# A weight-streaming kernel of two transformer blocks: low parts of two weight chunks in one VectorE instruction

## What is computed

```python
h = rms_norm(x, g_mix)
proj = h @ w_in
qa, ka, va, qr, kr, vr, gr, gate_a, gate_r = jnp.split(proj, pts, axis=-1)
oa = moba_attention(rms_norm(heads(qa, A_HEADS), q_gain), rms_norm(heads(ka, A_HEADS), k_gain), heads(va, A_HEADS))
orr = retention(heads(qr, R_HEADS), heads(kr, R_HEADS), heads(vr, R_HEADS))
orr = head_group_norm(orr)... * jax.nn.silu(gr)
merged = jax.nn.sigmoid(gate_a) * (oa @ w_o_attn) + jax.nn.sigmoid(gate_r) * (orr @ w_o_ret)
x = x + merged @ w_out
h2 = rms_norm(x, g_ffn)
g, u = jnp.split(h2 @ w_ffn_in, 2, axis=-1)
return x + (jax.nn.silu(g) * u) @ w_ffn_out
```

## Time and profile before

| | |
|---|---|
| median of three runs | 2584.09 us (2583.65 to 2584.09) |
| profiled execution | 2583.7 us, its span 2581.8 us |
| TensorE matmuls | 2568.1 us busy, 99% |
| TensorE weight loads | 2295.8 us, 89% |
| VectorE | 1634.9 us, 63% |
| ScalarE | 1326.9 us, 51% |
| GpSimd | 57.7 us, 2% |
| DMA | 507.39 MB, mean 197 GB/s |
| granted TensorE clock, mean | 0.999 of full speed |

### The profile page before, as it was taken

One profiled execution on the slowest core, in us unless ns is written; L12 is line 12 of the kernel. 1 busy time (PEld: TensorE's weight loads), 2 busy tenths in 40 slices (PEclk: granted clock), 3 DMA queues, 4 the chain that ended last, 5 costly groups with the idle time before them and its releaser, 6 DMA issues.

```text
span 2581.8 us, 38392 instructions
## 1 busy us (share of the span) xinstructions
PE 2568.1 (99%) x13844; PEld 2295.8 (89%) x13844; DVE 1634.9 (63%) x1721; ACT 1326.9 (51%) x1567; POOL 57.7 (2%) x55
## 2 busy tenths in 40 slices
PE   9999999999999999999999999999999999999998
PEld 8998888888889999999888898998889999998887
DVE  7568755556656656566655567667687776766555
ACT  6446665554445444444444466546564444444444
POOL 0000000000000000000000000000000000000000
PEclk9999999999999999999999999999999999999999
DMA  8666666667666666666666655664666666666664
GB/s 262 206 198 190 182 188 176 199 203 225 198 195 193 203 198 202 199 200 202 200 205 201 206 174 168 179 196 155 197 186 200 201 199 204 197 202 202 204 202 165
DMA packets 232229, 507.39 MB, mean 197 GB/s; under 512 B 15856, under 2 KB 16256, under 8 KB 231504
## 3 DMA queue, kind: packets, MB, share of 16 engines
q1 hardware_dynamic: 230272, 498.53, 63.9%
q0 software_dynamic: 1296, 6.88, 0.8%
q10 hardware_dynamic: 576, 0.82, 0.1%
HBM read 504.07 MB, written 2.10 MB: 196 GB/s over the span
## 4 chain that ended last, share of the span: by engine, by line
PE 99%; DVE 1%; DMA 0%; ACT 0%; SPq 0%; issue 0%; DVEq 0%
PE ps L405 31%; PE ps L414 16%; PE ps L416 16%; PE ps L415 16%; PE ps L406 15%; PE ps L478 1%; PE ps L734 0%; PE ps L727 0%; DMA raw<-w_in 0%; PE ps L797 0%; PE ps L550 0%; PE ps L583 0%; DVE wlo L1426 0%; PE ps L383 0%; PE ps L694 0%; PE ps L563 0%
## 5 line engine op out<-in xcount | busy, mean ns | idle before, releaser
L1426 DVE TENSOR_TENSOR wlo<-raw,whi 128x1024 fp32r<-128x1024 f32 x944 | 1169.8, 1243 | 892.4 <-ACT whi L867 883.0
L867 ACT ACTIVATE whi<-raw 128x1024 fp32r<-128x1024 f32 x943 | 996.3, 1058 | 1203.5 <-PE ps L406 597.7
L405 PE MATMUL ps<-hT,whi 128*128 128x512 f32 x3680 | 1208.6, 383 | 1.3 <-DVE hT L1475 0.6
L406 PE MATMUL ps<-hT,wlo 128*128 128x256 f32 x3680 | 1003.1, 273 | 0.0
L405 PEld LDWEIGHTS ps<-hT,whi 128*128 128x128 f32 x3680 | 695.5, 189 | 99.1 <-DVE hT L1475 1.5
L406 PEld LDWEIGHTS ps<-hT,wlo 128*128 128x128 f32 x3680 | 706.5, 192 | 0.2
L414 PE MATMUL ps<-whi,hT 128*128 128x512 f32 x1088 | 420.6, 387 | 0.0
L416 PE MATMUL ps<-whi,hT 128*128 128x512 f32 x1088 | 412.4, 379 | 0.0
L415 PE MATMUL ps<-wlo,hT 128*128 128x512 f32 x1088 | 412.3, 379 | 0.0
L414 PE MATMUL ps<-whi,split_e 128*128 128x512 f32 x832 | 316.2, 380 | 0.0
L415 PE MATMUL ps<-wlo,split_e 128*128 128x512 f32 x832 | 315.3, 379 | 0.0
(11 more groups left out here) (264 smaller groups left out, 1008.0 us busy)
## 6 DMA issues: line engine op xcount, KB each, us to landing
raw<-w_ffn_in SPq DMA_DIRECT2D x352, 512.0 KB, 4.2
raw<-w_in SPq DMA_DIRECT2D x303, 512.0 KB, 4.2
raw<-w_ffn_out SPq DMA_DIRECT2D x176, 512.0 KB, 4.6
raw<-w_o_ret SPq DMA_DIRECT2D x32, 512.0 KB, 4.7
raw<-w_out SPq DMA_DIRECT2D x32, 512.0 KB, 4.6
raw<-w_o SPq DMA_DIRECT2D x32, 512.0 KB, 4.0
raw<-w_o_attn SPq DMA_DIRECT2D x16, 512.0 KB, 4.6
resid<-x POOLq DMA_DIRECT2D x1, 2048.0 KB, 11.9
```

The costliest lines, as they stand in the source:

```text
L405: pe.matmul(acc, whi[:, c % SLOTS, f], in_turn(hT[:, kt, :, :]), start=(kt == 0), stop=False)
L406: mm = pe.matmul(acc[:, 0:SEQ], wlo[:, c % SLOTS, f], in_turn(hT[:, kt, 0, :]), start=False, stop=(kt == KT - 1))
L867: act.activation(whi[:, c % SLOTS, :], raw[:, c % SLOTS, :], ACT.Copy).then_inc(hi_ready, 1)
L1426: dve.tensor_tensor(wlo[:, c % SLOTS, :], raw[:, c % SLOTS, :], whi[:, c % SLOTS, :].bitcast(F32), ALU.subtract).then_inc(lo_ready, 1)
```

## The change

`ahead` on VectorE makes the low parts in twos. `split_two` waits until both high parts are there, makes 2048 columns with one instruction, and adds 2 to `lo_ready` when it ends, so both chunks are signalled to TensorE, and both raw slots to SyncE, at that moment. The pairs are (4, 5) and (6, 7) of this block and (0, 1) and (2, 3) of the next, made at the odd steps. `side` of the even step, which stood between the two splits, now stands ahead of both. With `hold`, step 6 is a single split, and the held one stays where it was. ScalarE, TensorE, GpSimd and SyncE have the same programs as before. In the changed file every line from the new function on stands 8 further down.

```diff
+            def split_two(blk, c):
+                dve.wait_ge(hi_ready, blk * CPB + c + 2)
+                two = slice(c % SLOTS, c % SLOTS + 2)
+                dve.tensor_tensor(wlo[:, two, :], raw[:, two, :], whi[:, two, :].bitcast(F32), ALU.subtract).then_inc(lo_ready, 2)
+
             def ahead(blk, side=nothing, more=True, hold=False):
 
                 side(-1)
                 for k in range(CPB):
                     if k < SLOTS:
-                        split(blk, k + SLOTS)
-                    elif more and not (hold and k == CPB - 1):
+                        if k % 2:
+                            split_two(blk, k - 1 + SLOTS)
+                    elif more and hold and k == CPB - 2:
                         split(blk + 1, k - SLOTS)
+                    elif more and not (hold and k == CPB - 1) and k % 2:
+                        split_two(blk + 1, k - 1 - SLOTS)
                     side(k)
```

## The result

| | before | changed |
|---|---|---|
| median | 2584.05 us (5 runs, 2583.35 to 2584.09) | 2611.7 us (5 runs, 2610.26 to 2612.17) |
| ratio | | 1.0108, 95% interval 1.0097 to 1.0119 |
| profiled execution | 2583.7 us, span 2581.8 | 2610.3 us, span 2608.4 |

The change costs 27.65 us, 1.1%. I had forecast 2601.7 us with a range of 2590 to 2611: the right way, with a loss of 17.6 instead of 27.65, and the measured time lies 0.7 above the range. The profiled execution is the fastest of the five, 26.6 us behind the one of before; it is the one that the traces explain. What makes the other executions up to 1.9 us longer is taken up at run e13, and stays open in part.

The account below looks back on a forecast made before the run. TensorE bounds the kernel, with VectorE's waits as slack. Places of 13.75 us and GpSimd's product of 3.9 add 17.6 to the profiled 2583.7, and the median lies 0.4 above: 2601.7 us, range 2590 to 2611.

Parts of the forecast that it names:

- What bounds the kernel, and the time of the instruction: TensorE bounds, busy 2568.1 of 2581.8 us, VectorE's waits are slack; the instruction of 2048 columns takes 2.29 us.
- The places: Single spots where TensorE misses a low part or a product behind a pair; their losses add to 13.75 us.
- Start: At the kernel's start chunk 4's low part comes with chunk 5's, at 21.6 instead of 19.33: +2.3 us.
- attention's output: Chunks 220 and 221 load late beside a 2 MB load of x, delaying the pair: +2.0 us (0.5 to 3).
- the head's output: VectorE's work for a head's output, behind pair (600, 601), reaches TensorE's L405 later: +1.05 us.
- retention's output: Two epilogues in retention's output whose products TensorE's L478 reads without spare time come 1.07 later: +2.1 us.
- GpSimd's product: Second FFN, 11 times: the product, taken as 2.4 not 3.11 us, blocks the pair; 0.35 each, +3.9 us (0 to 12).
- Their p: The p of the differential values, one of ten smaller places: +0.35 us.
- the clock: TensorE's pause at the start halves the granted clock for a while: +2 to +5 us, chance 0.05.
- The ring: Raw slots freed late and in twos make loads the bound: +5 to +18 us, 2607 to 2620, chance 0.07.
- Not slower: At every pair the wide instruction is cheap, 1.3 us or less: 2586 us, chance 0.04.
- absorbed: Late products aren't what TensorE waits for, leaving the start and little else: 2586 to 2589 us, chance 0.07.

Follow-up runs that it names:

- e13: The changed kernel with 11 matmuls without use in TensorE's pause ahead of chunk 4 at the start: 2610.4 us.
- e5: The changed kernel with the second FFN's product moved from GpSimd to VectorE, right behind the epilogue: 2605.4 us.
- e7: The changed kernel with single splits for chunks 4 and 5 of the blocks behind GpSimd's product, 12 pairs of 452: 2603.95 us.
- e2: Single instructions at their own steps as in the kernel before, but one joint signal for two chunks with the odd one: 2587.25 us.
- e3: Wide pairs only in the first block's FFN (33 of 118 blocks), single splits as before everywhere else: 2583.7 us.
- e8: Wide pairs only where the changed kernel's trace shows no stall (252 of 452), single splits elsewhere: 2583.8 us.
- e10: The changed kernel with one more wait on GpSimd, so its second FFN product starts after the pair behind it is made: 2604.9 us.
- e4: The changed kernel with single splits in the first half of the second block's FFN (22 blocks): 2601.6 us.
- e12: The changed kernel with the last pair of each block, ahead of the epilogue, as single splits: 2599.5 us.
- e9: The kernel before with every load held back by one chunk, VectorE unchanged: 2592.75 us.

## Why the prediction was right and wrong

**What bounds the kernel, and the time of the instruction**: right. 2.29 forecast, 2.29 measured; the quiet stretches are at 2.62 for a chunk, and the slack left to an even chunk is 1.58, forecast 1.7:

```profile
135.17 1.06 ACT L867 ACTIVATE whi<-raw 128x1024 fp32r<-128x1024 f32 x1 [1.56 <-PE ps L406]
...
136.34 2.29 DVE L1432 TENSOR_TENSOR wlo<-raw,whi 128x2048 fp32r<-128x2048 f32 x1 [2.95 <-ACT whi L867]
```

**The places**: nearly every one that I named is in the trace, and few that I didn't. Start, attention's output (whose size varies from one execution to the next) and the head's output are within 0.2. Most others cost more than I said. This is the term of the sum that I mis-sized first: **I charged a stall with a lateness of 1.07 us and nothing else, and a stall costs more.** Three small amounts were left out.

First, the pair also begins later. It starts 0.10 us after ScalarE's high part ends, where a single split starts 0.03 after (medians of the 383 pairs and the 674 splits of before that waited for ScalarE; 136.34 against 136.23 above, 126.40 against 126.37 in the earlier trace rows). With the 1.07 of the longer instruction that is 1.14. The changed kernel, turn of rows in retention's output:

```profile
660.84 1.22 DVE L1749 TENSOR_TENSOR area_d<-area_d,big 128x1024 f32<-128x1024 f32 x1
...
662.28 0.66 PE L478 MATMUL ps<-first,area_d 128*128 128x128 f32 x4 [0.98 <-DVEq L1751]
```

VectorE ends at 662.06. Before it was 653.68, and the kernel was 7.25 us behind by then: the product is 1.13 late, and so is TensorE, which follows after 0.22 as it did before. At the second turn the product is 1.50 late, and I can't say why. Second, of a low part TensorE takes 0.05 to start (2253.70 to 2253.75 above). Third, behind a wait the first matmul lasts 0.48 instead of 0.38, which 29 matmuls show in the changed kernel and not before, and where a low part was missing the next chunk starts 0.10 later than in a running stream. The rows had it: TensorE's matmul behind its one wait at 19.33 took 0.48. Over the places of the table but the convolution and their p, the measured column is 4.7 us above the forecast's, of the 9.0 by which the profiled execution is beyond the forecast.

**GpSimd's product**: the mechanism, the choice of 2.4 over 3.11 and the pair's length (4.3 forecast, 4.28 measured) were right, and each cost 0.57 instead of 0.35: 0.47 by which chunk 4 starts late, and 0.10 of restart. Over all 11 that is 6.1 instead of 3.9 us, part of the 4.7.

**The step that was missing**: the convolution, a term that the sum has at nothing and that costs 2.4. In each second block of the second FFN a pair stands behind eight instructions of it instead of four, since the even step's work now comes ahead of the pair:

```profile
2234.73 0.48 DVE L2110 SCALAR_TENSOR_TENSOR area_d<-temp,conv,area_d 128x256 f32<-128x256 f32 x1
2235.13 2.29 DVE L1432 TENSOR_TENSOR wlo<-raw,whi 128x2048 fp32r<-128x2048 f32 x1
```

It ends at 2237.42, and TensorE starts the chunk at 2237.47, 0.14 late, with 0.10 of restart. The forecast doesn't name this place: it goes by the slack of a quiet stretch, and here VectorE runs almost without a pause from one pair to the next. In e5 and e7 the 0.14 shrinks to 0.02 and the restart of 0.10 stays.

**Their p** (1.0 instead of 0.35) I read wrong by 0.6. The product there comes 1.75 late, which one pair's 1.14 doesn't explain; the cause stays open.

**The range**: its upper end of 2611 lies 0.7 under the median. It took single rivals in turn, and what came was the sum of small excesses nearly all of one sign. The forecast's own upper bound was also added up wrong: 1 and 2.5 on top of 2601.7 are 2605.2 and not 2606. The rival that I had given 0.05, **the clock**, came in part: I priced a fall at 2 to 5; it costs 1.6 to 1.8, and it came in three of six profiled executions with the pair at the start, though not in the changed kernel's own. That the pause of 2.8 was shorter than the 3 us at the end of the kernel was no protection.

**The ring** (rival 1) didn't come as a bound (e2, e3, e8), though ScalarE waits 230 us for loads now. **Not slower** and **absorbed** are out: no pair gained, and nearly all the named places lose.

## What to carry to other kernels

Where one engine is busy for 99%, merging instructions on another has next to nothing to gain and can lose: the merged instruction signals both halves at the end of the later one, and everything behind it comes late by the difference, here 1.1 us. Read such a change as a list of places and not as busy time, count each stall at its lateness plus the start and restart of the waiting engine (0.15 for a low part here), and merge only where the list has no entry (252 of 452 pairs here, at no cost and no gain). An engine pair that excludes each other, like VectorE's split and GpSimd's product, is worth an explicit order: one wait brought back 6.8 us (e10).

## What the runs showed of the hardware

A GpSimd product and a VectorE subtraction, both with SBUF inputs, exclude each other in either order: 2.37 and 2.29 us alone, 4.28 for the pair when it comes second, and 3.11 for the product when it does. The VectorE instruction of 2048 columns starts 0.10 us after the ScalarE instruction that it waits for, one of 1024 columns 0.03 after. After TensorE's pause at the start, 2.4 to 3.0 us long, the granted clock fell to 0.50 in three of six profiled executions (e5, e7, e10, but not in the changed kernel, e4 and e12), and was back some 3 us later. Further on it fell after pauses of 1.7 and 2.0 us in e12 and after one of 2.7 us in e9. A fall costs 1.6 to 1.8 us.
